# First projection blocks of a hybrid diffusion layer on one Trainium2 core: scale and shift loaded in turn, two blocks worked two rows of h at a time

## What is computed

```python
sh1, sc1, g1, sh2, sc2, g2 = jnp.split((jax.nn.silu(c) @ ada_w[l] + ada_b[l])[:, None, :], 6, axis=-1)
h = rmsnorm(x, norm1_g[l]) * (1.0 + sc1) + sh1
a_l, s_l, qkv_l = split_proj(h @ w_in[l])        # 1024 x 2816
u, v = jnp.split(jax.nn.gelu(s_l), 2, axis=-1)   # spatial gating: columns 768 to 1279
...
y = merge_heads(conv, gating, attention) ; x = x + g1 * y
h2 = rmsnorm(x, norm2_g[l]) * (1.0 + sc2) + sh2
x = x + g2 * peer_ffn(h2, ...)                   # queries, top 16 of 16384 experts, gather
```

## Time and profile before

| | |
|---|---|
| median of 3 runs | 977.26 us (977.19 to 981.38) |
| profiled execution | 976.05 us, of it 974.3 us span |
| PE busy | 911.8 us, 94% |
| DVE busy | 553.6 us, 57% |
| ACT busy | 259.6 us, 27% |
| POOL busy | 253.9 us, 26% |
| memory traffic | 292.74 MB, mean 300 GB/s |

### The profile page before, as it was taken

How to read it: one execution, slowest core, us unless ns; L and a number is a source line. 1 busy time by engine, 2 the same in 40 slices (tenths; PEclk the granted TensorE clock), 3 DMA queues, 4 the chain that set the end, 5 groups by cost and what they waited for, 6 DMA issues and landing times.

```text
span 974.3 us, 17939 instructions
## 1 busy us (share of the span) xinstructions
PE 911.8 (94%) x6850; PEld 839.1 (86%) x6850; DVE 553.6 (57%) x1155; ACT 259.6 (27%) x568; POOL 253.9 (26%) x239
## 2 busy tenths in 40 slices
PE   5799998889999999999998999999999999999996
PEld 3697997568898999998988999999998888888895
DVE  1455115757189949874547787784445454444523
ACT  2443233744534111112216666630000000000002
POOL 0000000410323053365441111138343333333200
PEclk9598999899999999999999999999999999999999
DMA  9664675033254689999999867679999999999981
GB/s 367 276 253 174 211 273 208 2 126 134 87 186 162 236 314 410 410 409 410 409 409 409 293 226 248 238 260 399 408 408 408 410 409 409 409 409 409 409 346 44
DMA packets 73984, 292.74 MB, mean 300 GB/s; under 512 B 9026, under 2 KB 9154, under 8 KB 67396
## 3 DMA queue, kind: packets, MB, share of 16 engines
q1 hardware_dynamic: 45508, 191.13, 50.6%
q0 software_dynamic: 28416, 100.78, 27.1%
HBM read 290.72 MB, written 1.05 MB: 299 GB/s over the span
## 4 chain that ended last, share of the span: by engine, by line
PE 48%; DMA 26%; ACT 2%; DVE 2%; issue 2%; POOL 1%; SPq 0%; DVEq 0%; ACTq 0%
PE bank L830 23%; DMA stage<-in_peer_v 20%; PE bank L886 12%; PE bank L839 4%; DMA A<-in_peer_u,row_expert 3%; DMA stage<-in_peer_u_t 2%; PE bank L573 1%; PE bank L574 1%; PE bank L575 1%; PE bank L727 1%; PE bank L724 1%; PE bank L726 1%; PE bank L779 1%; PE bank L757 1%; PE bank L699 1%
## 5 line engine op out<-in xcount | busy, mean ns | idle before, releaser
L886 PE MATMUL bank<-A,stage 128*128 128x160 f32 x2048 | 300.4, 303 | 11.1 <-DMA stage<-in_peer_v 2.7
L886 PEld LDWEIGHTS bank<-A,stage 128*128 128x128 f32 x2048 | 280.4, 190 | 31.0 <-DMA stage<-in_peer_v 29.3
L830 PE MATMUL bank<-A,stage 128*128 128x160 f32 x2048 | 289.2, 300 | 4.0 <-issue 2.3
L830 PEld LDWEIGHTS bank<-A,stage 128*128 128x128 f32 x2048 | 280.1, 190 | 7.4 <-issue 7.0
L1341 DVE SCALAR_TENSOR_TENSOR sum<-A,row_gate,sum 128x1024 f32<-128x1024 f32 x81 | 104.0, 1284 | 106.1 <-DMA A<-in_peer_v,row_expert 106.1
L1622 POOL DMA_INDIRECT A<-in_peer_u,row_expert x80 | 90.3, 1129 | 179.3 <-DVE row_dot L1328 167.0
L1328 DVE CUSTOM_DVE_ANT_0 A<-A 128x1024 f32<-128x1024 f32 x80 | 97.0, 1221 | 55.5 <-DMA A<-in_peer_u,row_expert 39.9
L1622 POOL DMA_INDIRECT A<-in_peer_v,row_expert x84 | 80.3, 956 | 133.0 <-DVE sum L1341 118.3
L1161 ACT ACTIVATE A<-bank 128x480 f32<-128x480 f32 x1 | 0.6, 571 | 273.8 <-PE bank L886 273.8
L575 PE MATMUL bank<-h_hi,ring_low 128*128 128x256 f32 x256 | 72.7, 284 | 0.0
L1108 ACT ACTIVATE A<-bank 128x160 f32 (+1 forms) x88 | 26.7, 304 | 160.0 <-PE bank L830 142.3
(11 more groups left out here) (234 smaller groups left out, 1243.6 us busy)
## 6 DMA issues: line engine op xcount, KB each, us to landing
stage<-in_peer_u_t SPq DMA_DIRECT2D x128, 512.0 KB
stage<-in_peer_v SPq DMA_DIRECT2D x128, 512.0 KB
A<-in_ada_w SPq DMA_DIRECT2D x24, 1024.0 KB, 7.5
A<-in_w_in SPq DMA_DIRECT2D x11, 1024.0 KB, 4.8
A<-in_w_q SPq DMA_DIRECT2D x8, 1024.0 KB, 5.3
A<-in_w_out SPq DMA_DIRECT2D x4, 1024.0 KB, 6.8
stage<-in_bias_mask SPq DMA_DIRECT2D x1, 2048.0 KB, 12.3
A<-in_peer_v,row_expert POOLq DMA_INDIRECT x84
```

Source lines behind the costliest of these rows:

```text
L830: mm = pe.matmul(o, stage[j][:, k * P:(k + 1) * P], H2[:, k, 0:ND], start=(k == 0), stop=(k == KD - 1))
L886: mm = pe.matmul(bank[b][:, n * ND:(n + 1) * ND], stage[c % SLOTS][:, m * P:(m + 1) * P], A3[:, c, :], start=(c == 0 and n == 0), stop=(c ...
```

## The change

`OWN` names `w_in` blocks 4 and 3. They leave the ring and get buffers of their own (in the space of YR and YS), for the raw block and in place for its low half. The `ada` blocks of scale and shift are loaded and worked in turn, one of each; each pair gives the gain and shift of two rows of h, and `scaled_h` scales and rounds these two rows at once. `in_part` i then does the matmuls of rows 2i and 2i + 1 for both blocks, in banks 6 and 7, between the `ada` pairs. ACT and DVE do the `split` of block 4 after the first pair of rows and that of block 3 after the second. SP loads the two blocks as the third and sixth. The constants of the gating and the context come later in SP's stream. The number of banks taken in turn changes with it, and with that the bank of several later steps.

```diff
+OWN = (("w_in", 4), ("w_in", 3))
...
-    for s in (SC1, SH1):
-        for b in range(4):
-            ada(4 * s + b)
-            if len(behind) > 1:
-                turn()
-    steps.append(("split", 0))
-    turn()
-    steps.append(("split", 1))
+    for i in range(4):
+        ada(4 * SC1 + i)
+        ada(4 * SH1 + i)
+        turn()
+        turn()
+        steps.append(("scaled_h", i))
+        if i < len(OWN):
+            steps.append(("split", i))
+        if i:
+            steps.append(("in_part", i - 1))
+    steps.append(("in_part", 3))
...
+    out = [b for b in out if b not in OWN]
+    for n, b in enumerate(OWN):
+        out.insert(3 * n + 2, b)
...
-    return out, [[b for b in out if b not in second], second]
+    return out, [[b for b in out if b not in second and b not in OWN], second]
...
+        elif kind == "in_part":
+            if n == 0:
+                for m, (matrix, b) in enumerate(OWN):
+                    put((matrix, b, 0), 6 + m)
+        elif (kind, n) in OWN:
+            pass
...
+        elif kind == "column" and n // 4 in (SC1, SH1):
+            put(("mod_part", n), sections[n // 4])
...
+        own = A[:, 8192:8192 + len(OWN) * KD * BLK].rearrange("p (s k n) -> p s k n", s=len(OWN), k=KD)
+        own_lo = own_low[:, :].rearrange("p (s k n) -> p s k n", s=len(OWN), k=KD)
...
-        weight_hi = [tile_hi[n % 2] for n in range(13)]
+        weight_hi = [tile_hi[0], out_hi3[:, :].rearrange("p (k n) -> p k n", k=KD)]
+        weight_hi += [tile_hi[(n + 1) % 2] for n in range(2, 13)]
...
-        hi_free = [None, None] + splits[:W_IN_BLOCKS] + [("w_in", 10), ("w_in", 10)]
+        hi_free = [None, None, None, splits[0]] + splits[2:W_IN_BLOCKS] + [("w_in", 10), ("w_in", 10)]
...
+                if (matrix, b) in OWN:
+                    sp.dma_start(raw((matrix, b)), sources[matrix][b]).then_inc(own_full[OWN.index((matrix, b))], 16)
...
-                if n == 2 * RING + 1:
+                if (matrix, b) in OWN:
+                    sp.dma_start(raw((matrix, b)), sources[matrix][b]).then_inc(own_full[OWN.index((matrix, b))], 16)
+                else:
+                    slot, second = ring_of[(matrix, b)], late((matrix, b))
+                    if slot >= RING:
...
+                early = s in (SC1, SH1)
+                if early:
+                    o = opened(pe, ("mod_part", b))
+                else:
+                    o = opened(pe, ("mod", s)) if b % 4 == 0 else bank[place[("mod", s)][0]]
...
+            def in_part(i):
+
+                (tokens_hi, tokens_lo), (dims_hi, dims_lo) = (split_weights(b) for b in OWN)
+                o = [opened(pe, b + (0,)) if i == 0 else bank[place[b + (0,)][0]] for b in OWN]
+                for k in (2 * i, 2 * i + 1):
+                    pe.wait_ge(h_ready, k + 1)
+                    for t in range(2):
+                        tt = slice(t * P, (t + 1) * P)
+                        products = [(h_hi[0][:, k, tt], tokens_hi[:, k, :]), (h_hi[0][:, k, tt], tokens_lo[:, k, :]),
+                                    (H_lo[:, k, tt], tokens_hi[:, k, :])]
+                        for n, (lhs, rhs) in enumerate(products):
+                            mm = pe.matmul(o[0][:, t * BLK:(t + 1) * BLK], lhs, rhs, start=(k == 0 and t == 0 and n == 0),
+                                           stop=(k == KD - 1 and n == 2), skip_group_check=True)
+                    if k == KD - 1:
+                        mm.then_inc(fill_sem(OWN[0] + (0,)), 1)
+                    for m in range(2):
+                        cc = slice(m * P, (m + 1) * P)
+                        products = [(dims_hi[:, k, cc], h_hi[0][:, k, :]), (dims_hi[:, k, cc], H_lo[:, k, 0:T]),
+                                    (dims_lo[:, k, cc], h_hi[0][:, k, :])]
+                        for n, (lhs, rhs) in enumerate(products):
+                            mm = pe.matmul(o[1][:, m * T:(m + 1) * T], lhs, rhs, start=(k == 0 and m == 0 and n == 0),
+                                           stop=(k == KD - 1 and n == 2), skip_group_check=True)
+                    if k == KD - 1:
+                        mm.then_inc(fill_sem(OWN[1] + (0,)), 1)
...
-                elif kind == "column" and n == 4 * SH1 + 3:
-                    round_h(0)
+                    landed(act, block_name)
+                    act.activation(weight_hi[n], raw(block_name), ACT.Copy).then_inc(weight_rounded, 1)
...
+            def modulation_part(b):
+
+                s, kk = b // 4, slice(2 * (b % 4), 2 * (b % 4) + 2)
+                c = 4 * (b % 4)
+                o = full(dve, ("mod_part", b))
+                bb = colv[:, COL_ADA_B + s * KD:COL_ADA_B + (s + 1) * KD][:, kk].unsqueeze(2).broadcast_to([P, 2, 2])
+                link(dve.tensor_tensor(mod[:, s, kk, :], o[:, c:c + 4].rearrange("p (k v) -> p k v", v=2), bb, ALU.add))
+                dve.sem_inc(free_sem(("mod_part", b)), 1)
+                if s == SC1:
+                    link(dve.scalar_tensor_tensor(gain1[:, kk, :], mod[:, SC1, kk, :], 1.0,
+                                                  colv[:, COL_N1:COL_N1 + KD][:, kk].unsqueeze(2)
+                                                  .broadcast_to([P, 2, 2]), ALU.add, ALU.mult))
+
+            def scale_h(part, of=range(KD)):
+
+                for k in of:
                     h = H[:, k, part * T:(part + 1) * T]
                     dve.tensor_scalar(h, h, gain1[:, k, part:part + 1], mod[:, SH1, k, part:part + 1], ALU.mult,
                                       ALU.add).then_inc(h_full, 1)
-                    if k:
+                    if k != of[0]:
                         rest_of_h(part, k - 1)
-                rest_of_h(part, KD - 1)
+                rest_of_h(part, of[-1])
...
+                elif kind == "column" and n // 4 in (SC1, SH1):
+                    modulation_part(n)
+                elif kind == "scaled_h":
+                    scale_h(0, (2 * n, 2 * n + 1))
```

More of the change, by code:

```diff
@@ L244, in bank_uses @@
                 put((kind, j), (1, 2, 3, 7)[j])
-        elif kind in ("squares", "split", "context", "ctx_squares", "yn", "quarter", "scores"):
+        elif kind in ("squares", "split", "context", "ctx_squares", "yn", "quarter", "scores", "scaled_h"):
             pass
@@ L489, in free_sem, with late, raw, low @@
             return bank_free[place[name][0]]
+        def late(block_name):
+            return block_name in rings[1]
+        def raw(block_name):
+            if block_name in OWN:
+                return own[:, OWN.index(block_name)]
+            return (WR2 if late(block_name) else WR)[:, ring_of[block_name] % RING]
+        def low(block_name):
+            if block_name in OWN:
+                return own_lo[:, OWN.index(block_name)]
+            return (WR2_lo if late(block_name) else WR_lo)[:, ring_of[block_name] % RING]
+        def landed(eng, block_name):
+            if block_name in OWN:
+                eng.wait_ge(own_full[OWN.index(block_name)], 16)
+            else:
+                n = ring_of[block_name]
+                eng.wait_ge(ring_full[late(block_name)][n % RING], 16 * (n // RING + 1))
         @block.sync
@@ L715, in out_projection @@
                 pe.wait_ge(quarter_split, 16)
-                w = [(weight_hi[splits.index(("w_out", b))], WR_lo[:, ring_of[("w_out", b)] % RING]) for b in range(4)]
+                w = [(weight_hi[splits.index(("w_out", b))], low(("w_out", b))) for b in range(4)]
                 for k in range(KD):
@@ L797, in _ @@
                     spread(n)
+                elif kind == "in_part":
+                    in_part(n)
+                elif (kind, n) in OWN:
+                    pass
                 elif kind == "w_in":
@@ L950, in _, with round_h @@
             act.wait_ge(eps_ready, 1)
-            def round_h(part):
-                for k in range(KD):
+            def round_h(part, of=range(KD)):
+                for k in of:
                     act.wait_ge(h_full, KD * part + k + 1)
@@ L995, in _ @@
                     block_name = splits[n]
-                    slot = ring_of[block_name]
-                    late = block_name[0] == "w_q"
                     if hi_free[n]:
@@ L1204, in modulation @@
                 dve.sem_inc(free_sem(("mod", s)), 1)
-            def scale_h(part):
-                for k in range(KD):
+            def modulation_part(b):
[10 more added lines that the diff above has]
+            def scale_h(part, of=range(KD)):
+                for k in of:
                     h = H[:, k, part * T:(part + 1) * T]
```

64 lines of the change are left out of this document (26 added, 38 removed).

## The result

| | before | after |
|---|---|---|
| median of 4 runs each | 977.91 us (977.19 to 981.38) | 983.75 us (982.80 to 987.79) |
| profiled execution | 976.05 us, span 974.3 | 987.79 us, span 986.0 |

The ratio is 1.0062 with an interval of 1.0036 to 1.0088: the change makes the kernel slower by 0.6%, 6.1 us (3.5 to 8.6). The profiled execution of after is the slowest of its four and that of before is faster than the four measured beside it, so the two traces lie 11.7 us apart, twice the distance of the medians. Which part belongs to the change has to be read from more than one pair.

The account below looks back on a forecast made before the run. PE was taken as the main bound, half of the chain of waits, so early delays reach the end. Terms 1.5 + 0.3 + 2.6 + 2.6 = +7.0 us on 976.05, plus 1.2 to the median, gave 984.3; range 977.5 to 990.5.

Parts of the forecast that it names:

- The early part: Start up to block 1: block 1 starts at 57.65 instead of 56.16, +1.5 us.
- Block 10 in bank 2: Block 10 must wait until the first group sum is out of its bank: +0.3 us, at most 0.6.
- The wait of the first query block: First query block in bank 2 waits for the second of ACT's four copies, till 249.3: +2.6 us.
- The clock behind the pause: First query block: after PE's idle time the clock is low for 6.0 us, +2.6 us, between 0 and 3.3.
- the clock holding at the query block: Rival: PE keeps full clock after the pause at the first query block, 981.7 us; chance 0.15.
- The clock falling between bursts: Rival: later `in_part` bursts at low clock, 2.4 us more each; 989.1 for two, 991.5 for three; chance 0.17.
- The rule of the Trainium skill: Short bursts between waits start at low clock every time, so the second to fourth `in_part` would all be slow.
- The delay absorbed at the end: Rival: transfers set the pace in the last 300 us, so a late PE costs nothing, 977.3 us; chance 0.10.
- The change not doing what it says: Rival: the first `in_part` starts at 26.0, once block 4 is split, 6.5 us earlier; 977.8 us; chance 0.04.

Follow-up runs that it names:

- again: The changed kernel unaltered, run once more against the kernel before: 986.09 us, ratio 1.0048.
- banks back: The changed kernel with the turn of the banks moved on by two, so later steps have their old banks: 981.54 us, ratio 1.0005 against before.
- bank alone: The kernel before with only the turn of the banks moved on by two at the first query block: 984.40 us, ratio 1.0036.
- bank filled: The kernel before with the first query block's bank changed and ten unread matmuls in PE's pause ahead of it: 981.23 us, ratio 1.0023.
- parts last: The changed kernel with all four `in_part` behind the last `ada` pair: 985.83 us, ratio 1.0069 against before.
- split first: The changed kernel with the `split` of block 1 ahead of block 4's gelu on ACT: 984.91 us, ratio 1.0043 against before.
- all three: The changed kernel with banks moved back, block 1's `split` moved ahead and all `in_part` behind the last `ada` pair: 976.01 us, ratio 0.9977 against before.

## Why the prediction was right

The forecast was 984.3 us, slower, with 0.66 on slower. The median is 983.75 and the ratio stands for 6.1 us where the sum had 7.0. The mechanism of every term was found in the traces. Two terms were right in size, the early one was perhaps too large, and that of the clock was too large by 1 us.

| step | forecast | trace of after |
|---|---|---|
| low halves end | 26.0, 32.5 | 25.94, 31.97 |
| first `in_part` starts | 32.5 | 32.08 |
| third pair starts | 37.8 | 37.47 |
| second and third `in_part` start | 41.0, 46.8 | 40.74, 46.74 |
| `split` of block 1 starts | 53.3 | 53.32 |
| block 1 starts | 57.65 | 57.59 |
| PE idle before the first query block | 4.9 | 4.89 |
| low clock behind it | 6.0 | about 3.5 |

- **The early part, +1.5.** The way there is confirmed within 0.6 us at each step: one wait for both blocks' low halves, two `ada` pairs queued behind it, ACT's `split` behind block 4's gelu. As a size it depends on the execution. The traces of after, again and banks back have block 1 at 56.7 on average, those of before, bank alone and bank filled at 55.7: +1.0. At the group sums the same averages are 147.7 and 146.3, and at the copies 250.6 and 249.2: +1.4 both times. The growth from 1.0 to 1.4 comes from the trace of before alone, which was at the low clock for a shorter time there (last section). So the traces show about 1.0 to 1.4. Banks back, which holds this part alone, gives 0.5 us with an interval of -1.3 to 2.4: the size fits, but a cost above zero is not shown by the times.
- **Block 10 in bank 2, +0.3.** Measured 0.3. The block begins at 150.63, right behind the start of DVE's reciprocal at 150.57. Its second matmul (one line of the timeline of before, two of after) starts 1.91 us behind the start of the group sums before and 2.22 after:

```profile
147.57 0.28 PE L574 MATMUL bank<-ring_low,h_hi 128*128 128x256 f32 x1
```

```profile
148.60 1.96 PE L780 MATMUL bank<-A,con 128*128 128x512 f32 x4 [0.18 <-ACT A L1132]
...
150.82 0.28 PE L619 MATMUL bank<-ring_low,h_hi 128*128 128x256 f32 x1
```

  The five kernels with the old bank take 1.90 to 1.91 us, the four with bank 2 take 2.22, and the 0.3 is still there 37 matmuls later.
- **The wait of the first query block, +2.6.** Measured 2.6 (copies to keys, bank filled against before).
- **The clock behind the pause, +2.6.** The mechanism is right: 0.50 behind 4.89 us of waiting, 1.00 when the pause is filled. The size was not. I let the low clock last 6.0 us from the first matmul, as it did from 38.3 to 44.3. Here it had fallen near 249.8, inside the pause, so 3.3 us of the low stretch passed while PE was idle and cost nothing. The matmuls began at 253.09, and a window of 254 to 258 at 0.68 is 2.6 us at 0.50 and the rest at 1.00, so it rose near 256.6, 3.5 us after the start. The 48 matmuls took 7.36 us instead of 5.85, 1.5 more; the experiment gives 1.6. (The upper bound of 3.3 was a slip: by the same rows 7 us at the low clock cost 3.2.) The step that failed is the size of this term: it took what was left of one low stretch behind a pause as what is left behind every other.

With these sizes the sum is 1.4 + 0.3 + 2.6 + 1.6 = 5.9 us, or 5.5 with 1.0 for the early part. The two measurements of the change gave 6.1 and 4.7.

One reading of the rows of before was wrong, the one in favour of the clock holding at the query block: behind the pause of 1.11 us PE went on at 23.79 at full clock for 0.2 us only, then the clock fell. The chance of 0.15 had nothing else for it. The window just behind, before:

```profile
24.10:26.50 2.40, 2.40 (x20) 1.36 (x12) 0.00 (x0) 0.38 (x1) 0.00 (x0) 0.50 1.02 420
```

**The rivals.** The clock holding at the query block (981.7) is out by its windows. The clock falling between bursts is out as well: the windows of after have 1.00 from 40 to 60, and the second `in_part` takes 3.0 us (40.74 to 43.78), as at full clock. The rule of the Trainium skill that I set against this (TensorE: Matmul & The Clock Gate, section "HAM oscillation — how this bites in real kernels") speaks of bursts with long waits for transfers between them; here `ada` matmuls filled most of the room, and the trace shows no slow burst behind the first. The delay absorbed at the end is out: with the same early part, the kernels with and without the bank fault differ by 4.2 us (4.7 and 0.5, intervals apart), close to what the bank costs by the keys. The change not doing what it says is out: the first `in_part` starts at 32.08, not at 26.0.

**The 11.7 us between the two profiled executions** come apart in the table: 1.4 up to block 1, 1.5 up to the group sums, 0.8 up to the copies, 4.2 up to the keys, 0.1 up to the experts and 3.7 in the experts. Of the third, 0.3 is block 10. The second and the last are mostly not shown to be the change's: bank alone, whose start is that of before, takes 90.8 from block 1 to the group sums and 666.3 from the experts to the end, where before took 89.5 and 660.5. The trace of before is the fastest of the nine in both. Its mean granted clock, 0.978, was reached by none of the 34 runs of before in the first group and by five of the 23 in the second. It was a lucky execution, and a single pair of traces would have charged its luck to the change.

## What to carry to other kernels

Where resources are handed out in turn, here four accumulator banks, taking two users out of the turn gives later steps another one. List what each later step waits for after such an edit, however far away it stands: this coupling, 200 us behind the edit, cost more than the edit itself (4.2 us against 1.0 to 1.4 in the traces), and one line put it right. And a single wait for two inputs also holds back all that is queued behind it; moving that wait back alone gained 0.5 us at block 1, and with the next thing in the queue, a `split` behind another engine's work, moved as well, 5.1 against before. That the second move is what made the first pay is not shown by itself: there is one trace of each, and the clock was low in the first.

## What the runs showed that I had not expected

**The clock fell after a short pause, in some executions.** PE waits 1.88 us for the column and 0.39 for block 1. In the trace of after the clock stays at 1.00. In again, banks back and parts last, with the same two waits, it falls to 0.50 soon behind block 1's first matmul, for some 3 us. One window of banks back:

```profile
57.00:58.00 1.00, 1.00 (x6) 1.00 (x6) 0.93 (x3) 1.00 (x1) 0.00 (x0) 0.50 0.51 205
```

In split first and all three, where the first wait is 1.21 and 0.59 us, it holds. So an idle time of two microseconds, alike in the timeline, may or may not cost the clock in a given execution.

**Most of what the traces differ by in two stretches is time at the low clock.** From block 1 to the group sums every kernel runs the same matmuls (736 to 740 records). The windows of that stretch in before and in parts last:

```profile
56.16:145.66 89.50, 88.33 (x736) 78.55 (x737) 34.57 (x41) 30.62 (x40) 0.00 (x0) 0.96 0.60 223
```

```profile
55.93:150.50 94.57, 92.50 (x736) 81.01 (x737) 34.59 (x41) 30.63 (x40) 0.00 (x0) 0.91 0.56 203
```

The other stretch lies between the two expert tables, from the first matmul of the gates (line 839 before, 914 after) to the first of the second table. Its first 10 us in before and in bank alone:

```profile
516.48:526.48 10.00, 9.75 (x75) 9.54 (x76) 6.38 (x18) 5.74 (x17) 0.94 (x1) 1.00 1.03 410
```

```profile
524.41:534.41 10.00, 9.75 (x52) 9.54 (x53) 4.71 (x13) 2.81 (x9) 0.94 (x1) 0.70 1.03 409
```

From the clock record of each trace, in us:

| kernel | block 1 to group sums | of it at 0.50 | PE idle before the gates | gates to second table | of it at 0.50 |
|---|---|---|---|---|---|
| before | 89.5 | 6.8 | 2.5 | 132.1 | 0 |
| after | 91.0 | 10.2 | 2.5 | 133.8 | 3.4 |
| after, again | 91.1 | 10.2 | 5.6 | 133.7 | 3.2 |
| banks back | 90.9 | 10.2 | 5.0 | 134.6 | 5.0 |
| bank alone | 90.8 | 10.2 | 5.8 | 135.0 | 5.9 |
| split first | 91.8 | 10.2 | 4.4 | 134.4 | 4.7 |
| parts last | 94.6 | 17.1 | 4.8 | 134.2 | 4.2 |
| all three | 90.8 | 10.2 | 2.5 | 132.1 | 0 |
| bank, filled | 91.6 | 10.2 | 4.1 | 134.6 | 5.5 |

In both stretches a microsecond at 0.50 costs about half a microsecond. In the first, 10.2 us more of it cost parts last 5.1 us against before. In the second the times follow it almost exactly, from 132.1 with none to 135.0 with 5.9. So the 3.5 us that parts last lost behind block 1, and 1.3 of the 1.8 us that all three edits gave back, are low clock. So are 1.6 of the 3.7 us by which the first trace of after is longer in the experts.

PE's idle time before the gates is 2.5 us in three traces and 4.1 to 5.8 in six, and neither the bank nor the order of the start sorts them. In the six it ends with DVE, whose products of gathered expert rows stand in front of its part of the gates. What decides this wait, and how long the clock stays low in a given execution, is open: there is one trace of each kernel. The low clock isn't the whole spread between executions either. One run of before had a mean granted clock of 0.926, against 0.971 to 0.976 in the 33 beside it, and took 985.89 us, only 5 us above their median.
